# A 31-tap depthwise convolution: four tiles on TensorE as four time phases by 32 channels, three tiles on VectorE, one on GpSimd

## What is computed

```python
def causal_dwconv(x, w, b):          # K = 31 taps, 1024 channels
    K, C = w.shape
    y = lax.conv_general_dilated(
        x, w[:, None, :], window_strides=(1,), padding=[(K - 1, 0)],
        dimension_numbers=("NWC", "WIO", "NWC"), feature_group_count=C)
    return y + b

def conformer_conv(x, norm, w1, b1, dw_w, dw_b, ln_g, ln_b, w2, b2):
    h = rms_norm_2(x, norm) @ w1 + b1
    h = jax.nn.glu(h, axis=-1)
    h = causal_dwconv(h, dw_w, dw_b)
    h = jax.nn.silu(layer_norm_2(h, ln_g, ln_b))
    return h @ w2 + b2
```

## Time and profile before

| | us |
|---|---|
| median of 3 runs | 1747.32 |
| the profiled execution, its time | 1746.16 |
| the profiled execution, its span | 1744.3 |
| TensorE busy in the span | 1732.0 |
| VectorE, ScalarE, GpSimd busy | 1307.7, 1016.9, 99.2 |

### The profile page before, as it was taken

One profiled execution on the slowest core, in us unless ns is written; L12 is line 12 of the kernel. 1 busy time (PEld: TensorE's weight loads), 2 busy tenths in 40 slices (PEclk: granted clock), 3 DMA queues, 4 the chain that ended last, 5 costly groups with the idle time before them and its releaser, 6 DMA issues.

```text
span 1744.3 us, 24250 instructions
## 1 busy us (share of the span) xinstructions
PE 1732.0 (99%) x9134; PEld 1493.1 (86%) x9134; DVE 1307.7 (75%) x1747; ACT 1016.9 (58%) x1406; POOL 99.2 (6%) x154
## 2 busy tenths in 40 slices
PE   9999999999999999999999999999999999999998
PEld 7888888888888888888889988888888988888887
DVE  7797677665877686766669787788778987588775
ACT  6775647454666655644555865655456656555544
POOL 1000000000000000000000000500003360000000
PEclk9999999999999999999999999999999999999999
DMA  9656655566765565565666564455665515356553
GB/s 318 203 155 188 182 158 157 170 193 189 235 194 165 168 181 169 157 181 170 192 194 198 183 193 145 149 189 189 187 193 182 170 37 182 124 166 192 187 188 108
DMA packets 209476, 308.71 MB, mean 177 GB/s; under 512 B 11664, under 2 KB 112656, under 8 KB 209104
## 3 DMA queue, kind: packets, MB, share of 16 engines
q1 hardware_dynamic: 207232, 299.50, 56.3%
q0 software_dynamic: 2128, 7.66, 1.3%
HBM read 306.07 MB, written 1.05 MB: 176 GB/s over the span
## 4 chain that ended last, share of the span: by engine, by line
PE 94%; DVE 3%; ACT 1%; issue 1%; DMA 0%; SPq 0%; DVEq 0%; ACTq 0%
PE bank L1711 52%; PE bank L1776 26%; PE bank L2178 3%; PE bank L1743 3%; PE bank L2227 2%; PE bank L1826 1%; DVE weights_lo L1060 1%; PE bank L1840 1%; PE bank L2099 1%; PE bank L2117 1%; PE bank L1809 1%; PE bank L1848 0%; PE bank L2023 0%; PE bank L1988 0%; PE bank L2071 0%
## 5 line engine op out<-in xcount | busy, mean ns | idle before, releaser
L1060 DVE TENSOR_TENSOR weights_lo<-weights_raw,weights_hi 128x1024 fp32r<-128x1024 f32 x560 | 668.3, 1233 | 221.2 <-ACT weights_hi L581 216.1
L581 ACT ACTIVATE weights_hi<-weights_raw 128x1024 fp32r<-128x1024 f32 x559 | 574.4, 1056 | 391.0 <-DMA weights_raw<-in_w_in_dram 184.6
L1711 PE MATMUL bank<-weights_hi,h_parts 128*128 128x512 f32 x1856 | 567.0, 391 | 0.3
L1711 PEld LDWEIGHTS bank<-weights_hi,h_parts 128*128 128x128 f32 x1856 | 348.0, 188 | 73.4 <-DVE h_parts L1492 0.6
L1711 PE MATMUL bank<-weights_lo,h_parts 128*128 128x512 f32 x928 | 347.5, 389 | 0.0
L1776 PE MATMUL bank<-h_parts,weights_hi 128*128 128x512 f32 (+1 forms) x1248 | 302.7, 384 | 1.4 <-ACT arena L601 0.7
L1711 PE MATMUL bank<-weights_hi,arena_parts 128*128 128x512 f32 x928 | 270.0, 390 | 0.0
L1776 PEld LDWEIGHTS bank<-h_parts,weights_hi 128*128 128x128 f32 x1248 | 219.8, 189 | 41.1 <-DVE arena L1114 1.3
L1711 PEld LDWEIGHTS bank<-weights_lo,h_parts 128*128 128x128 f32 x928 | 174.3, 188 | 35.4
L1711 PEld LDWEIGHTS bank<-weights_hi,arena_parts 128*128 128x128 f32 x928 | 173.6, 188 | 35.4
L1776 PEld LDWEIGHTS bank<-h_parts,weights_lo 128*128 128x128 f32 x1248 | 169.4, 190 | 11.1
(11 more groups left out here) (310 smaller groups left out, 1640.4 us busy)
## 6 DMA issues: line engine op xcount, KB each, us to landing
weights_raw<-in_w_in_dram SPq DMA_DIRECT2D x224, 512.0 KB, 3.7
weights_raw<-in_f_w_up_dram SPq DMA_DIRECT2D x96, 512.0 KB, 3.5
weights_raw<-in_f_w_down_dram SPq DMA_DIRECT2D x48, 512.0 KB, 3.6
weights_raw<-in_w_up_dram SPq DMA_DIRECT2D x40, 512.0 KB, 3.6
weights_raw<-in_c_w_pw_dram SPq DMA_DIRECT2D x24, 512.0 KB, 3.6
weights_raw<-in_ab_w_in_dram SPq DMA_DIRECT2D x20, 512.0 KB, 3.7
weights_raw<-in_w_out_dram SPq DMA_DIRECT2D x16, 512.0 KB, 3.6
weights_raw<-in_xa_wk_dram SPq DMA_DIRECT2D x16, 512.0 KB, 3.4
```

The source lines that it names most:

```text
L581: nc.scalar.activation(w_hi[:, q % SPLIT, 0:w], raw[:, n % RAW, 0:w], ACT.Copy).then_inc(hi_done, 1)
L1060: tt(w_lo[:, n % RAW, 0:w], raw[:, n % RAW, 0:w], w_hi[:, q % SPLIT, 0:w].bitcast(F32), ALU.subtract)\
L1711: return mm(bs[t][:, :], sp_[:, 2 * u + kk, t * P:(t + 1) * P], wp[:, kk, :], start=first and u == us[0] and kk == 0 and n == 0, stop=last ...
```

## The change

TensorE now convolves the four tiles 4 to 7 whole, VectorE tiles 0, 1 and 2, GpSimd tile 3.

For TensorE a tile is rearranged. Its 128 channels are four groups `g` of 32, its 256 time steps four phases `i` (time modulo 4) of 64. `deal` (on TensorE) moves, for each group, phase `i` of its 32 channels to partitions 32i to 32i + 31: four f32 matmuls per group, whose stationary operand is a slice of `wsT` that is 128, 96, 64 or 32 columns wide, and which stream 64 time steps of stride 4. ScalarE copies the result to SBUF behind eight zero columns (`dealt`). The convolution of one group is then nine matmuls (`LAGS`), 128 by 128, each streaming 64 columns. The host lays out the 4 x 4 x 9 matrices, 9.4 MB (`conv_phases`). Those of tiles 4 and 5 are fetched through GpSimd's queue (2.36 MB each) in stage X0 and at the end of F0, in place of the diagonals; those of tiles 6 and 7 through SyncE's queue into the same place, group by group, as TensorE is done with the group before. ScalarE evicts each tile with 16 instructions of 32 partitions by 64 columns, output stride 4. The ring of products shrinks from 8 to 6. `glu3` comes ahead of the second tap of VectorE's second chain, and not ahead of the fourth.

```diff
-        CONV_PE = (5, 7, 6)
-        SHARED, KEPT = 7, 14
-        CONV_DVE, CONV_POOL = ((0, 1), (2, 4)), 3
-        DIAG = {5: (18, 20), 6: (8, 10), 7: (14,)}
-        TAPS = [(CONV_POOL, d) for d in range(1, 31)] + [(SHARED, d) for d in range(KEPT, 31)]
-        RING = 8
-        def diag(ft, d):
-            return sec(DIAG[ft][d // 16], 2)[:, d % 16 * P:(d % 16 + 1) * P]
+        CONV_PE = (4, 5, 6, 7)
+        CONV_DVE, CONV_POOL = ((0, 1), (2,)), 3
+        TAPS = [(CONV_POOL, d) for d in range(1, 31)]
+        RING = 6
+        LAGS, HALO = 9, 8
+        AREA = {4: (sec(18, 4), sec(14)[:, 0:512]), 5: (sec(8, 4), sec(14)[:, 512:1024])}
+        def phases(ft):
+            at = {4: 0, 5: 288, 6: 576}.get(ft)
+            t = sec(23)[:, 512:800] if at is None else sec(15)[:, at:at + 288]
+            return t.rearrange("p (g n) -> p g n", g=4)
+        def moved(g, i):
+            return wsT[:, g, 96 - 32 * i:P]
+        def phase_matrix(ft, n):
+            return AREA[4 + ft % 2][n // 32][:, n % 32 * P:(n % 32 + 1) * P]
...
-                      + pick("cb", 2) + pick("ca", 2) + pick("y", 1) + pick("cb", 3) + pick("ca", 3) + pick("cv", *CONV_PE)
+                      + pick("cb", 2) + pick("ca", 2) + pick("y", 1) + pick("cb", 3) + pick("ca", 3) + pick("dl", 4, 5) + pick("cv", 4) + pick("dl", 6, 7) + pick("cv", 5, 6, 7)
...
+                if n == PC.unit_at(("ca", 3), "C") + RAW:
+                    for i in range(2):
+                        for g in range(4):
+                            sp.wait_ge(pe_done, PC.at(("group", 4 + i, g), "C"))
+                            o = 4608 * (2 + i) + 9 * P * g
+                            if g < 3:
+                                sp.dma_start(AREA[4 + i][0][:, 9 * P * g:9 * P * (g + 1)], A["conv_phases"][:, o:o + 9 * P])\
+                                    .then_inc(later_in[i][g], 16)
+                                continue
+                            sp.dma_start(AREA[4 + i][0][:, 27 * P:32 * P], A["conv_phases"][:, o:o + 5 * P]).then_inc(later_in[i][g], 16)
+                            sp.dma_start(AREA[4 + i][1], A["conv_phases"][:, o + 5 * P:o + 9 * P]).then_inc(later_in[i][g], 16)
...
-            def diagonals(ft, ds):
-                for d in ds:
-                    c = COL_C + 48 + 8 * (30 - d) + ft
-                    ins = nc.gpsimd.tensor_scalar(diag(ft, d), ident, cols2[:, c:c + 1], 1.0, ALU.mult, ALU.mult)
-                ins.then_inc(pool_done, GC(f"diag{ft}{ds[0]}"))
...
-            diagonals(5, range(31))
-            diagonals(SHARED, range(KEPT))
+            def phase_weights(n, ft):
+                for dst, a, b in zip(AREA[ft], (0, 4096), (4096, 4608)):
+                    pool.dma_start(dst, A["conv_phases"][:, 4608 * n + a:4608 * n + b]).then_inc(phase_in[n], 16)
+            phase_weights(0, 4)
             pool.wait_ge(pe_done, PC.at(("o", 3), "F0"))
-            diagonals(6, range(31))
+            phase_weights(1, 5)
+            pool.wait_ge(pe_done, PC.at(("hT", 3)))
+            for ft in CONV_PE:
+                nc.gpsimd.memset(phases(ft)[:, :, 0:HALO], 0.0).then_inc(pool_done, GC())
+            nc.gpsimd.memset(wsT[:, :, :], 0.0).then_inc(pool_done, GC())
+            pool.wait_ge(pool_done, GC.n)
+            for g in range(4):
+                q = slice(32 * g, 32 * g + 32)
+                nc.gpsimd.tensor_copy(wsT[q, g, 96:P], ident[q, q])\
+                    .then_inc(pool_done, GC(*(["moves"] if g == 3 else [])))
+                pool.wait_ge(pool_done, GC.n)
             for n, (ft, d) in enumerate(TAPS):
                 if n == 0:
                     pool.wait_ge(act_done, SC.at(f"tap{CONV_POOL}"))
-                if d == KEPT and ft == SHARED:
-                    pool.wait_ge(act_done, SC.at(f"cv{SHARED}"))
...
-                for ft in ((0, 1), (2, 3), (4,), ())[q]:
+                for ft in ((0, 1), (2, 3), (), ())[q]:
...
-            products(18, 30)
+            def dealt(ft):
+                act.wait_ge(pe_done, PC.at(("dl", ft)))
+                b = bank(SC, "dl", ft)
+                link(nc.scalar.activation(phases(ft)[:, :, HALO:HALO + 64], b[:, 0:S].rearrange("p (g n) -> p g n", g=4), ACT.Copy),
+                     ("free", "dl", ft), f"dealt{ft}")
+            dealt(4)
+            dealt(5)
+            products(18, 22)
+            dealt(6)
+            dealt(7)
+            products(22, 30)
             v = rows_of(14)
-            for ft in CONV_PE:
-                b = filled("cv", ft)
-                link(nc.scalar.activation(feat(16, 2)[:, ft, :], b[:, 0:S], ACT.Identity,
-                                          bias=cols2[:, COL_C + 24 + ft:COL_C + 25 + ft]), ("free", "cv", ft), f"cv{ft}")
-                if ft == 5:
-                    act.wait_ge(vec_done, VC.at(f"glu{SHARED}"))
-                    products(30, 36)
-                if ft == SHARED:
-                    products(36, len(TAPS))
+            for n, ft in enumerate(CONV_PE):
+                act.wait_ge(pe_done, PC.at(("cv", ft)))
+                b = bank(SC, "cv", ft)
+                for g in range(4):
+                    for j in range(4):
+                        c = COL_PH + 4 * n + g
+                        y = feat(16, 2)[32 * g:32 * g + 32, ft, :].rearrange("p (n j) -> p j n", j=4)[:, j, :]
+                        nc.scalar.activation(y, b[32 * j:32 * j + 32, 64 * g:64 * g + 64], ACT.Identity,
+                                             bias=cols2[32 * j:32 * j + 32, c:c + 1])\
+                            .then_inc(act_done, SC(*([("free", "cv", ft), f"cv{ft}"] if (g, j) == (3, 3) else [])))
...
-                dve.wait_ge(act_done, after_act(f"tap{CONV_DVE[i][1]}"))
+                dve.wait_ge(act_done, after_act(f"tap{CONV_DVE[i][-1]}"))
...
-                        dve.wait_ge(vec_done, VC.n - 1)
+                        dve.wait_ge(vec_done, VC.n - 1 if len(CONV_DVE[i]) > 1 else VC.n)
...
-                if d == 4:
+                if d == 2:
...
-            for ft in CONV_PE:
-                taps = KEPT if ft == SHARED else 31
-                pe.wait_ge(pool_done, GC.at(f"diag{ft}0"))
+            pe.wait_ge(pool_done, GC.at("moves"))
+            def deal(ft):
                 pe.wait_ge(vec_done, VC.at(f"glu{ft}"))
+                b = begin("dl", ft)
+                x = feat(2, 2)[:, ft, :].rearrange("p (n i) -> p i n", i=4)
+                for g in range(4):
+                    for i in (3, 2, 1, 0):
+                        ins = mm(b[0:32 * i + 32, 64 * g:64 * g + 64], moved(g, i), x[:, i, :], start=i == 3, stop=i == 0,
+                                 skip_group_check=True)
+                end(ins, "dl", ft)
+            deal(4)
+            deal(5)
+            for n, ft in enumerate(CONV_PE):
+                if ft == 5:
+                    deal(6)
+                    deal(7)
+                if ft == 7:
+                    mu(0, 1, 4)
+                pe.wait_ge(act_done, SC.at(f"dealt{ft}"))
+                if n < 2:
+                    pe.wait_ge(phase_in[n], 32)
                 b = begin("cv", ft)
-                for d in range(taps):
-                    ins = mm(b[:, d:S], diag(ft, d), feat(2, 2)[:, ft, 0:S - d], start=d == 0, stop=d == taps - 1,
-                             skip_group_check=True)
-                end(ins, "cv", ft)
-                if ft == SHARED:
-                    mu(0, 1, 5)
-            mu(3, 2, 4, 7, 6)
+                for g in range(4):
+                    if n >= 2:
+                        pe.wait_ge(later_in[n - 2][g], 16 if g < 3 else 32)
+                    for lag in range(LAGS):
+                        ins = mm(b[:, 64 * g:64 * g + 64], phase_matrix(ft, LAGS * g + lag), phases(ft)[:, g, HALO - lag:HALO - lag + 64],
+                                 start=lag == 0, stop=lag == LAGS - 1)
+                    ins.then_inc(pe_done, PC(*([("group", ft, g)] if n < 2 else []), *([("cv", ft)] if g == 3 else [])))
+            mu(5, 2, 3, 6, 7)
...
+def conv_phases(np, w):
+    got = np.zeros((4, 32, 4, 4, 9, 4, 32), np.float32)
+    taps = np.reshape(w[:, 512:], (31, 4, 4, 32))
+    c = np.arange(32)
+    for lag in range(9):
+        for i in range(4):
+            for j in range(4):
+                d = 4 * lag + j - i
+                if 0 <= d <= 30:
+                    got[i, c, :, :, lag, j, c] = np.transpose(taps[30 - d], (2, 0, 1))
+    return got.reshape(P, 4 * 4 * 9 * P)
```

More of the change, by code:

```diff
@@ L138, in build @@
         ident_r = sb("ident_parts", [P, P], F32R)
-        cols2 = sb("vector_columns_2", [P, 616])
+        cols2 = sb("vector_columns_2", [P, 632])
         brow = sb("row_vectors", [P, 2048])
@@ L160, in build @@
         brow_in, win_in, ws_in, out_done = (sem(n) for n in ("brow_in", "win_in", "ws_in", "out_done"))
+        phase_in = [sem(f"phase{i}_in") for i in range(2)]
+        later_in = [[sem(f"phase{i}_{g}_in") for g in range(4)] for i in (2, 3)]
         memT_in = [sem(f"memT{i}_in") for i in range(3)]
```

(14 more changed lines are left out.)

2 lines of the change are left out of this document (1 added, 1 removed).

## The result

The kernel after the change takes 1804.85 us (median of 4 runs, 1804.21 to 1805.71), the kernel before beside it 1747.41 us (4 runs, 1746.96 to 1748.67): 1.033 times as long, 95% interval 1.0317 to 1.0343, or +57.4 us. Forecast were +15.2 us and 1754.6 to 1771 us. The direction was right, the size was not, and the time lies outside the range.

A forecast was written before the change was run, and what follows sets the result against it. TensorE was taken as the bound: deals 5.0 + wait 2.7 + bands 32.2 + deals 5.0 + mean 3.4 + tail 1.6 from 1388.05 gave 1438.0 against 1422.52; less 0.3, +15.2 us, median 1762.5, range 1754.6 to 1771.

The forecast's parts named there:

- the price of the banded records: TensorE's banded matmuls: 288 records at 112 ns each, set by the load of 128 columns, 32.2 us.
- Rival (2): TensorE's records cost their stream, 57 ns, not their load; ScalarE then bounds; 1745.1 us or 1743.8; chance 0.10.
- the deals: TensorE's rearranging matmuls for tiles 4 to 7: 2.5 us a tile, 10.0 us for four.
- the slope: TensorE's weight loads: 0.86 ns a column, so deal records of 128, 96, 64, 32 columns cost 112, 85, 58, 57 ns.
- a rival with a chance of 0.10: Rival on TensorE's deals: width changes drain the array or strided reads halve the stream, pitch 120 ns; up to 1775 us.
- Rival (3): TensorE's granted clock falls to 1.2 GHz because the array streams only half of the time; 1800 us, chance 0.04.
- the tail: TensorE idles before the mean's last matmul for tile 7's 16 ScalarE evictions, 0.20 us apart: 1.6 us.
- the wait for `dealt4`: TensorE, after dealing tiles 4 and 5, idles until ScalarE has copied tile 4, before its bands: 2.7 us.
- what was costed at nothing: VectorE's taps, GpSimd's work, SyncE's queue waits and the matrix transfers were to delay TensorE by 0 us.
- the 0.3: After the stretch, VectorE's four subtractions run faster because GpSimd has finished: -0.3 us.

The follow-up runs named there:

- the kernel with wide deals: The kernel after, with every dealing matmul zero-padded to 128 stationary columns instead of 128, 96, 64 and 32; 1769.89 us.

## Why the prediction was right in its direction and wrong in its size

**Right: the price of the banded records, which their stream does not set.** 111 to 112 ns in after at full clock and in three experiments, for the 112 forecast; 32.1 us for 31.1 removed. The Trainium skill, TensorE: Matmul & The Clock Gate, section Back-to-back issue gap, has 25 ns in its table for a single matmul of up to 64 columns, and 81 ns at 128 columns for a sustained stream of loads and matmuls; the f32 records read here are 111 to 116 ns apart at full clock, at 64 and at 128 columns, so here the measurement decides. Rival (2) is out, since it needed a pitch below 65. That it is the load of 128 columns which sets the price, as the prediction has it, is less sure: no banded record with a narrower load was run, and the deals' records with loads of 32 columns come no sooner.

**Wrong: the deals, 10.0 us, of which after's full-clock price is 21.3.** Two steps failed. The first is "By the slope, records cost 112, 85, 58 and 57 ns". The slope was taken from how long loads last, between 36 and 128 columns, and used for how soon the records follow each other; the runs show 0.12 us at 128, 96, 64 and 32 columns alike. The one row with a narrow load, 100 and 36 columns in alternation, 0.12 us apart, could not tell: those records stream 256 columns, and so do the full-width ones of the projection, which are as far apart (46.09 us for 387). Without changes the deals cost 14.9 us: 4.9 of the miss. The second is "Widths below 128 may change the shape of the array in use; 100 and 36 in alternation start 0.12 us apart with no extra". It was taken as evidence against, the change priced at nothing in the forecast, and the +5 left to a rival with a chance of 0.10. Measured are 48 pauses of 0.15 to 0.19 us, 6.4 us beyond an undisturbed pitch: the rival's size was right, its chance was not. The Trainium skill, TensorEngine Tiling (Array Packing), section Key Properties, says that a change of tiling mode drains TensorE. The traces are in keeping with it where the width goes from 96 to 64, to 32 and back to 128, 0.15 to 0.21 us each, and show nothing between 128 and 96; that the pause is this drain isn't shown. Why the alternation of 100 and 36 in the trace of before showed no pause isn't settled; those are one-pass matmuls that stream 256 columns, and no run separates what of this matters.

**Wrong, and the largest: the clock.** The forecast put the clock at 1.00 throughout, and its reason for doubt was only the stream. Rival (3) named the outcome within 5 us (1800) and gave it 0.04, for a reason that is not enough: "because the array streams only half of the time". Two kernels with the same streams and the changes of width gone or rarer keep 1.00. That its number came so near is luck: it put some 40 us on the clock, where the clock has 27 and the deals, the pauses and the tail the rest. What the runs show is a chain: pauses at changes of width, between thin streams, take the clock down within some 5 us of deals; the bands that follow, which at full clock would have kept it there, keep it at half instead. By the difference between after and the kernel with wide deals, 35.9 us of span: 2.3 before the stretch, 6.4 the pauses themselves, and 27 the halved clock, of which 22.1 are the bands, 4.1 the deals and 1.1 the mean. The prediction had two rivals, drain and clock, with 0.10 and 0.04, and priced them as if they were independent; here the first brings the second with it. Before the clock fell, the load engine was busy for 3.17 of 5.00 us, where before has 31.66 in 34.47; that such a share would lower it, no row of before could have told. Why the clock falls with the pauses and not with the thin stream alone is shown only as far as these runs go; what the chip measures is not.

**Wrong in part: the wait for `dealt4`, 2.7 us.** ScalarE's copy ended 7.95 us into the stretch; forecast was 1395.7 - 1388.05 = 7.65. That reading of ScalarE and GpSimd held to 0.3 us. But the slower deals took 11.84 us and hid it, so the term is 0.

**Wrong in size: the tail, 1.6 us.** The place and the releaser were right (L2252 waiting for ScalarE's L1053). The evictions are 6.22/16 = 0.39 us apart and not 0.20: "468 ns for 256 columns from a bank, 172 for 2, so about 245 ns at 64" measured 366, of which 61 are the stride, and the overlap of 0.1 us between neighbours, taken from the products, did not exist for them (0.366 long, 0.39 apart). The stall of 4.5 us also lowers the clock of the first `v` matmuls: the part after the stretch is 2.0 us longer in after and in the kernel with wide deals alike, where the table of stretches has, right behind the stretch,

```profile
1444.00:1449.00 5.00, 5.00 (x13) 3.87 (x13) 3.97 (x6) 2.34 (x4) 0.00 (x0) 0.50 0.00 0
```

The forecast had nothing for this.

**Right: what was costed at nothing.** VectorE ends its taps at 1417.6, GpSimd its adds at 1438.9, SyncE's waits and the transfers hold up nothing in the stretch. VectorE's four subtractions take 2.86 us instead of 5.06 with GpSimd silent, as foreseen. GpSimd ends some 20 us later in the stretch than forecast, since its last products stand behind the slow deals, but the mean asks for its tile only at 1472.96.

**The account.** 15.2 + 4.9 (no narrow discount) + 6.4 (pauses) + 2.9 (tail) - 2.7 (hidden wait) + 2.3 (clock after the tail's idle, the 0.3 being already in) + 27.3 (clock in the stretch) = 56.3 us. With the stretch's later start, 3.0 us in this execution, that is 59.3 of the span's 59.6; the medians differ by 57.4, because the profiled after lies 0.9 us above its median and the profiled before 1.2 below that of its runs. Without the halved clock it would have been 15.2 + 11.5 = 26.7, by this estimate some 1774 us, and still 3 us above the range.

## What to carry to other kernels

Count records, each with its weight load, before streamed columns: here an f32 record with a load of its own cost 0.11 to 0.12 us, whether it streamed 64 or 128 columns and whether its stationary operand was 32 or 128 wide, so a packing that divides the columns by four and almost doubles the records gains nothing, and a reordering on TensorE comes on top of it. Give consecutive matmuls one stationary width, by padding with zeros if need be, or at least group them by width. When a mechanism makes TensorE pause often, price the clock together with it, and ask of the work that follows whether it is dense enough to bring the clock back. A fetch that is moved ahead of its use needs a place where the DMA engines are free, not just one that is early.

## What the runs showed of the hardware that was not expected

- A change of stationary width from 96 to 64, 64 to 32, and 32 to 128 columns stopped the weight loads for 0.15 to 0.21 us at full clock and made the matmuls 0.13 us later on average; from 128 to 96 nothing of it.
- Matmul records of 128, 96, 64 and 32 stationary columns with 64 streamed columns of stride 4 started 0.12 us apart alike; only the loads themselves are shorter.
- The granted clock kept the level that it had: f32 records with 64 streamed columns ran 48 us at 1.00 where they found it there, 111 to 116 ns apart, and 46 us in two pieces at 0.50 where they did not, 214 ns apart; with 128 columns they brought it back.
- 4.5 us of idle TensorE were followed by some 5 us at a clock of 0.50 to 0.68, and the rest of the kernel took 2.0 us longer than before.
- A ScalarE eviction of 32x64 from a bank takes 305 ns, 366 with every fourth column written, against 468 for 128x256.
- Two transfers of 2 MB and 1 MB requested together took the DMA share to 1.08 and held a weight unit back by 4.4 us; with the 2 MB alone the longest such wait was 1.9 us, and TensorE did not stand.
